# An output-projection schedule at a kernel's end: three old output tiles moved ahead, between conv and gating groups

## The chip, the cores and the metric

The kernel runs on all 8 cores of one Trainium2 chip. Each core takes one prompt sequence of 2048 tokens and 64 of the 512 sample tokens; the cores share nothing and exchange nothing. The metric is the device time of the slowest core in microseconds (us). In every core TensorE (PE) multiplies matrices, VectorE (DVE), ScalarE (ACT) and GpSimd (POOL) do the elementwise work, and SyncE (SP) issues most DMAs of activations. Each engine executes its own instructions strictly in the order in which the program lists them and waits on semaphores for results of the others.

## The reference, cut to what matters

```python
h = rms_norm(x, g_norm) * (1 + scale) + shift          # shift, scale, gate from silu(c) @ w_ada + b_ada
p = h @ w_in                                           # (T, 1024) @ (1024, 3584)
h_a, b_a, c_a, z_a, u_b, v_b, z_b = split(p)           # seven pieces of width 512
s = c_a * h_a                                          # group A: short gated convolution
conv = w[0] * s[t-2] + w[1] * s[t-1] + w[2] * s[t]
y_a = b_a * conv * silu(z_a)
v_n = layer_norm(v_b)                                  # group B: spatial gating, chunks of 128 positions
y_b = u_b * (tril(w_s) @ v_n + b_s) * silu(z_b)
y = concat([y_a, y_b]) @ w_out                         # (T, 1024) @ (1024, 1024)
out = rms_norm(x + gate * y, g_final)
# further outputs: the last two rows of s (new conv state), v_n of the sample tokens
```

## The kernel before

The 16 tiles of 128 prompt tokens of a core, and one tile of 64 sample tokens, are worked off in five blocks: `BLOCKS = ((4, False), (4, False), (3, True), (3, False), (2, False))`, tiles and whether the sample tile is in it. The last block (index 4) has two tiles, so its matmuls stream 256 columns; block 3, `PV` there, has three tiles.

Activations are kept transposed: `hT` holds 8 slices of 128 features. For a block the program records, in this order:
- four conv groups j = 0 to 3 (`A1`, `A2`). `A1` multiplies h and C (8 matmuls each, L477); ACT copies h out of its bank (L506), DVE forms s (L514), ACT takes the first tap (L525), DVE the other two (L532, twice). `A2` multiplies B and z; DVE gates (L546), ACT takes the silu (L550), POOL writes slice j of `yT` (L551).
- `V`: the v projection with its layer norm (L592, L607 to L622), within the conv groups; in the last block behind group 1.
- four gating groups (`GB`): U and z matmuls (16, L477), silu on ACT (L644), product on DVE (L647), the mixing matmuls (L656), their scaling on DVE (L666), and POOL writes slice 4 + j of `yT` (L676).

The output projection runs one block late. For an old tile, `C_mm` is 16 matmuls of 512 columns into two banks (L704); `C_s1` multiplies by the gate (DVE, L720 and L721) and adds x (DVE, L723; x comes by a DMA into `xc`, recorded by `C_load`, all three at once by `first_c`); `C_sq` sums the squares on ACT (L733); `C_s2` makes the reciprocal root in two steps on one number per row, L791 and then POOL's power (L793); `C_s3` scales the tile on DVE (L802) and SP stores it (L317). `cq` is the list of tiles of which `C_s3` is still to come; at the start of the last block a prompt tile of block 2 and its sample tile are in it.

In the last block before the change, old tile j (j = 0, 1, 2) goes behind gating group j. Then come the block's own two tiles: tile 0 (`C_mm` over slices 0 to 6 and then slice 7, `C_s1`, `C_s2`, `C_s3`), and tile 1 in two halves of 512 output columns (L743, `C_end1` L759 and L761, squares L763, `C_end2` L774, L776, L781), whose stores end the kernel. A `C_mm` over slices 0 to 6 is one recorded step: it waits at its first matmul until all seven slices are there.

The order on each engine is this recorded order; there is no planner. The recorder `Sched` adds a semaphore wait wherever a step reads or overwrites what another engine's step wrote or reads. Banks (8), `tmp` (9), `xc` (3) and `ob` (3, the output tiles) are handed out in rotation.

Of the kernel before, what the change touches and what calls it, by code (L numbers as in the profile page):

```python
# [7 lines left out]
ALU = mybir.AluOpType  # L8
AF = mybir.ActivationFunctionType

EPS = 1e-6
NCORES = 8
D = 1024
# [177 lines left out]
def build_nc(limit=None):  # L191
# [36 lines left out]
    def op(eng, fn, r=(), w=(), dma=False):  # L228
        return S.op(eng, fn, reads=r, writes=w, dma=dma)
# [96 lines left out]
    for b, (nt, smp) in enumerate(BLOCKS):  # L326
        B = Blk()
# [250 lines left out]
    def V2():  # L578
        while vlate:
            vlate.pop(0)()  # L580
# [202 lines left out]
               r=[("oh", n), sres, "gf_bc"], w=[("oh", n)])  # L783
            store(y_p[rows, sl], o[:, sl], [("oh", n)], ("out_y", B.i, i, n))

    def C_s2(B, i):
        ti, P, kind = B.tiles[i]
        R = slice(64, 128) if kind == "s" else slice(0, 128)
        o, ores, st, sres = cst[(B.i, i)]
        ss, rs = st[:, 0:1], st[:, 1:2]  # L790
        op("dve", lambda e: e.tensor_scalar(out=rs, in0=ss, scalar1=1.0 / D, scalar2=EPS, op0=ALU.mult, op1=ALU.add),  # L791
           r=[sres], w=[sres])
        op("pool", lambda e: e.tensor_tensor(out=rs, in0=rs, in1=mhalf[:, 0:1], op=ALU.pow),  # L793
           r=[sres, "mhalf"], w=[sres])
# [151 lines left out]
    cq = []  # L946
# [12 lines left out]
    def nxp(f, i, *a):  # L959
        if NX is not None and i < len(NX.tiles):  # L960
            f(NX, i, *a)

    for b in range(nb):
        B = PB[b]
        NX = PB[b + 1] if b + 1 < nb else None
        PV = PB[b - 1] if b > 0 else None
        N2 = PB[b + 2] if b + 2 < nb else None
        npv = len(PV.tiles) if PV is not None else 0
        last = NX is None
        late = b < 2  # L970

        def first_c():
            for i in range(min(NXC, npv)):
                C_load(PV, i)

        if last:
            for i in range(len(B.tiles)):
                C_load(B, i, i)
        for j in range(4):
            if not late:  # L980
                if j < 2:
                    nxp(prep_load, j + 2)
            A1(B, j)
            if b == 0 and j == 3:
                V2()
            if not late:
                nxp(prep_sq, j + 1)
            elif j == 3 and b == 1:
                nxp(prep_sq, 2)
                nxp(prep2, 0, "act")  # L990
            if j < 2 and cq and not last:
                C_s3(*cq.pop(0))
                if cq:
                    C_s2(*cq[0])
            A2(B, j)
            if last and j == 2 and cq:
                C_s3(*cq.pop(0))
                if cq:
                    C_s2(*cq[0])
            if not late:  # L1000
                nxp(prep2, j, "act")
                nxp(prep_xn, j + 1)
            if b == 0 and j == 0:
                late_loads_1([("spadB", 0)])
            if b == 1 and j == 0:
                wblk_ops()
            if j == 2 and b > 1:
                first_c()
            if b == 1 and j == 2:
                nxp(prep_sq, 0)  # L1010
                nxp(prep_sq, 1)
            if j == (1 if last else 2):
                V(B, (lambda: nxp(prep_xn, 0)) if b == 1 else None)
                if b > 0:
                    V2()
            if b == 0 and j == 2:
                wt_ops()
            if b == 0 and j == 3:
                nxp(prep_sq, 0)
                nxp(prep_sq, 1)  # L1020
                bias2_ops()
                nxp(prep_xn, 0)
                nxp(prep_xn, 1)
            if b == 1 and j == 2:
                nxp(prep_xn, 1)
                nxp(prep_load, 2)
                nxp(prep_load, 3)
            if b == 1 and j == 3:
                nxp(prep2, 1, "act")
                nxp(prep_xn, 2)  # L1030
        if not late and N2 is not None:
            for i in range(2):
                prep_load(N2, i)
        if b == 1:
            gate_ada()
            for q in range(NXC):
                S.alias(("xc", q), [("wada", 0), ("wada", 1), ("wada", 2), ("xa", 4), ("xa", 5)])
            for q in range(NOB):
                S.alias(("o", q), [("wada", 0), ("wada", 1), ("wada", 2), ("xa", 4), ("xa", 5)])
            first_c()  # L1040
        if not last:
            newconv(B)
        for j in range(4):
            if last:
                GB(B, j, (lambda j=j: C_sq(PV, j - 1)) if 0 < j <= npv else None)
                if j > 0:
                    C_s2(PV, j - 1)
                if j < npv:
                    C_mm(PV, j, 0, 8)
                    C_s1(PV, j, False)  # L1050
                if j == 0:
                    newconv(B)
                    while cq:
                        C_s3(*cq.pop(0))
                elif j < 4:
                    C_s3(PV, j - 1)
                continue
            if not late and not last:
                prep3(NX, [2 * j, 2 * j + 1])
            if b == 1 and j == 0:  # L1060
                nxp(prep_sq, 3)
            if b == 1 and j >= 2:
                prep3(NX, range(4 * j - 8, 4 * j - 4), "both")
            if j == 3 and N2 is not None and b > 0:
                prep_xn(N2, 0)
            GB(B, j)
            if b == 0 and j == 1:
                nxp(prep2, 0, "act")
                nxp(prep2, 1, "dve")
                nxp(prep_sq, 2)  # L1070
                nxp(prep_sq, 3)
                nxp(prep_xn, 2)
                nxp(prep_xn, 3)
            if b == 0 and j == 2:
                nxp(prep2, 2, "act")
                nxp(prep2, 3, "dve")
                prep3(NX, range(8), "both")
            if b == 1 and j < 2:
                nxp(prep2, 2 + j, "act")
                if j == 0:  # L1080
                    nxp(prep_xn, 3)
                prep_load(N2, j)
            if j < npv:
                C_step(PV, j, (PV, j + NXC) if j + NXC < npv else None)
            if j == 2 and N2 is not None and b > 0:
                prep_sq(N2, 0)
        if b == 0:
            for k in range(8):
                S.alias(("yT", 1, k), [("wada", 3), ("xa", 6), ("xa", 7)])
            late_loads_2([("win", 22, 0)])  # L1090
        if last:
            C_mm(B, 0, 0, 7)
            C_mm(B, 0, 7, 8)
            C_s1(B, 0)
            C_mm_half(B, 1, 0)
            C_end1(B, 1, 0)
            C_s2(B, 0)
            C_mm_half(B, 1, 1)
            C_end1(B, 1, 1)
            C_s3(B, 0)  # L1100
            C_end2(B, 1)
# [60 lines left out]
```

How the kernel before makes its waits and increments, by code:

```python
        def run(e, eng):  # L113
            seen = {}
            nw = 0
            for o in streams[e]:
                need = {}
                waits = list(o.deps)
                if o.is_dma and o.prev is not None:
                    waits.append(o.prev)
                for d in waits:
                    key = d.sem.num
                    if key not in need or need[key][1] < d.val:
                        need[key] = (d.sem, d.val)
                for key, (sem, val) in need.items():
                    if seen.get(key, 0) >= val:
                        continue
                    eng.wait_ge(sem, val)
                    seen[key] = val
                    nw += 1
                ins = o.fn(eng)
                if o.is_dma:
                    ins.then_inc(o.sem, 16)
                elif o.needed:
                    ins.then_inc(o.sem, 1)
            stats[e] = (len(streams[e]), nw)
# [18 lines left out]
            @block.sync  # L155
            def _(eng):
                run("sp", eng)
                for q in self.QUEUES:
                    last = {}
                    for o in streams[q]:
                        if o.is_dma:
                            last[o.sem.num] = (o.sem, o.val)
                    for sem, val in last.values():
                        eng.wait_ge(sem, val)
```

## Time and profile before

| | us |
|---|---|
| median of 3 runs (lowest, highest) | 343.68 (343.39, 365.61) |
| the profiled execution | 343.48 |
| its span on the slowest core (6), and on the fastest (1) | 341.7 and 338.1 |
| PE busy in the span | 287.9 (84%) |
| DVE busy | 186.5 (55%) |
| ACT busy | 122.0 (36%) |
| POOL busy | 110.6 (32%) |

The profile is of one execution, on its slowest core. The span runs from that core's first to its last instruction; 1.8 us of the execution's time lie around it. Times in rows are us from the span's start. Matmuls are pipelined, so a row of PE gives a group from its first start to its last end, and groups overlap by some 0.2 us. Neighbouring instructions of DVE likewise overlap by up to 0.1 us; where a sum is made, the distance from start to start is what counts.

### The profile page before, as it was taken

To read this page: it belongs to the slowest core of one execution; us is meant where nothing else is said; L and a number is where in the kernel's file an instruction comes from. 1 tells how busy PE (TensorE), PEld (TensorE's weight loads), DVE (VectorE), ACT (ScalarE), POOL (GpSimd) and SP (SyncE) were. 2 spreads that over 40 slices of the span, in tenths; PEclk is the share of its full clock that TensorE was granted. 3 is DMA by queue.
4 is the path that set the end of the run, shared out by engine and by line. 5 is a ranking of instruction groups with operands and counts; after the bars stand their busy time and mean duration, and the time that the engine had idled before them with its cause. 6 is when DMAs were issued, how large, how long until landed. Compare 5 with 4: busy or idle time off the path is not lost.

```text
span 341.7 us, 5602 instructions; the slowest of 8 cores (338.1 to 341.7 us)
## 1 busy us (share of the span) xinstructions
PE 287.9 (84%) x1767; PEld 151.4 (44%) x1792; DVE 186.5 (55%) x350; ACT 122.0 (36%) x215; POOL 110.6 (32%) x161
## 2 busy tenths in 40 slices
PE   0324639997799999999999999999999999999840
PEld 0222324443444445444455454446555557765410
DVE  0321015444564454846778836468863666667982
ACT  2611024207452234723445262443415244232320
POOL 7293065214423431412226342121432112222210
PEclk9999959999999999999999999999999999999995
DMA  5999999999999973193122715111180102527223
GB/s 130 214 166 165 170 160 146 176 160 257 204 213 182 228 131 94 31 255 118 62 92 93 205 44 149 61 63 62 61 238 11 33 0 94 154 70 195 90 111 124
DMA packets 14157, 44.51 MB, mean 130 GB/s; under 512 B 1968, under 2 KB 2352, under 8 KB 13104
## 3 DMA queue, kind: packets, MB, share of 16 engines
q0 software_dynamic: 6624, 21.24, 34.7%
q1 hardware_dynamic: 7504, 22.91, 22.2%
q8 instruction: 15, 0.25, 0.3%
q14 instruction: 14, 0.11, 0.1%
HBM read 51.02 MB, written 8.85 MB: 175 GB/s over the span
## 4 chain that ended last, share of the span: by engine, by line
PE 54%; DMA 24%; DVE 9%; issue 6%; POOL 3%; ACT 2%; DVEq 1%; POOLq 0%; SPq 0%; ACTq 0%
PE pb L477 31%; PE pb L704 12%; DMA win_bf<-win_l 12%; DMA wada<-wada_l 10%; PE pb L592 7%; DMA xc<-x_p 2%; DVE ob L802 2%; PE pb L403 2%; PE pb L656 1%; PE pb L814 1%; POOL xa L314 1%; DVE ob L723 1%; DVE tmp L532 1%; DVE ob L720 1%; DVE ob L721 1%
## 5 line engine op out<-in xcount | busy, mean ns | idle before, releaser
L477 PE MATMUL pb<-hT,win_bf 128*128 128x512 bf16 (+3 forms) x672 | 125.6, 341 | 4.1 <-DVE hT L410 1.8
L477 PEld LDWEIGHTS pb<-hT,win_bf 128*128 128x128 bf16 x680 | 66.0, 98 | 59.1 <-issue 4.9
L704 PE MATMUL pb<-wout_bf,yT 128*128 128x512 bf16 (+1 forms) x246 | 56.8, 379 | 2.7 <-POOL yT L676 1.2
L477 PE MATMUL pb<-hT,wh 128*128 128x512 bf16 (+3 forms) x277 | 53.9, 355 | 3.6 <-ACT hT L419 3.6
L676 POOL TENSOR_TENSOR yT<-tmp,tmp 128x512 bf16<-128x512 f32 (+3 forms) x20 | 22.0, 1098 | 67.7 <-DVE tmp L666 37.0
L551 POOL TENSOR_TENSOR yT<-tmp,tmp 128x512 bf16<-128x512 f32 (+3 forms) x20 | 23.7, 1185 | 58.0 <-DVE tmp L546 41.1
L733 ACT ACTIVATE junk<-ob 128x1024 bf16<-128x1024 f32 (+1 forms) x16 | 16.9, 1057 | 71.5 <-DVE ob L723 58.7
L477 PEld LDWEIGHTS pb<-hT,wh 128*128 128x128 bf16 x280 | 27.7, 100 | 27.9 <-issue 7.9
L532 DVE SCALAR_TENSOR_TENSOR tmp<-spad,pv,tmp 128x512 f32<-128x512 f32 (+2 forms) x40 | 26.3, 658 | 20.3 <-ACT tmp L525 13.1
L704 PEld LDWEIGHTS pb<-wout_bf,yT 128*128 128x128 bf16 (+1 forms) x256 | 23.9, 98 | 29.3 <-issue 2.4
L592 PE MATMUL pb<-wv_bf,hT 128*128 128x512 bf16 (+1 forms) x133 | 29.6, 379 | 0.2
L419 ACT ACTIVATE hT<-hT,shT,aT 128x384 bf16<-128x384 bf16 (+2 forms) x28 | 18.0, 694 | 26.3 <-DVE aT L468 25.4
L525 ACT ACTIVATE tmp<-spad,pv 128x512 f32<-128x512 f32 (+2 forms) x20 | 12.7, 636 | 38.4 <-DVE spad L514 29.7
L389 DVE TENSOR_SCALAR xn<-xa,stat 128x1024 bf16<-128x1024 f32 (+1 forms) x17 | 12.8, 755 | 24.5 <-POOL stat L382 24.4
L403 PE MATMUL pb<-ident,xn 128*128 128x128 bf16 (+1 forms) x136 | 11.5, 238 | 16.9 <-DVE xn L389 16.9
L514 DVE TENSOR_TENSOR spad<-pb,tmp 128x512 f32<-128x512 f32 (+2 forms) x20 | 11.7, 585 | 22.5 <-PE pb L477 11.0
L647 DVE TENSOR_TENSOR tmp<-pb,tmp 128x512 f32<-128x512 f32 (+3 forms) x20 | 11.9, 595 | 19.7 <-ACT tmp L644 19.7
L802 DVE SCALAR_TENSOR_TENSOR ob<-ob,stat,gf_bc 128x1024 f32<-128x1024 f32 (+1 forms) x16 | 20.5, 1280 | 1.5 <-POOL stat L793 1.4
L723 DVE TENSOR_TENSOR ob<-ob,xc 128x1024 f32<-128x1024 f32 (+1 forms) x15 | 18.4, 1225 | 4.7 <-DMA xc<-x_p 2.4
L378 ACT ACTIVATE junk<-xa 128x1024 bf16<-128x1024 f32 (+1 forms) x17 | 17.9, 1053 | 7.4 <-DMA xa<-x_p 7.0
L592 PEld LDWEIGHTS pb<-wv_bf,hT 128*128 128x128 bf16 (+1 forms) x136 | 13.3, 99 | 15.6 <-issue 0.4
L622 ACT ACTIVATE vn_bf<-pb,stat 128x512 bf16<-128x512 f32 x16 | 11.2, 774 | 24.2 <-DVE stat L616 12.8
(88 smaller groups left out, 261.1 us busy)
## 6 DMA issues: line engine op xcount, KB each, us to landing
y_p<-ob SPq DMA_DIRECT2D x15, 512.0 KB, 2.7
xc<-x_p SPq DMA_DIRECT2D x14, 512.0 KB, 7.8
wada<-wada_l POOLq DMA_DIRECT2D x6, 1024.0 KB, 36.0
xa<-x_p POOLq DMA_DIRECT2D x10, 512.0 KB, 40.1
win_bf<-win_l POOLq DMA_DIRECT2D x17, 256.0 KB, 43.5
xa<-x_p SPq DMA_DIRECT2D x8, 512.0 KB, 6.6
wout_bf<-wout_l POOLq DMA_DIRECT2D x2, 1024.0 KB, 60.4
wh<-winh_l POOLq DMA_DIRECT2D x4, 256.0 KB, 27.5
```

What stands on the lines that cost most here:

```text
L378: op("act", lambda e: e.activation(out=junk[0:P, :], in_=xa[ra][0:P, :], func=AF.Square, accum_out=ss), r=[("xa", ra)], w=[sres, "junk"])
L403: ii = pe.transpose(out=tv[:, k, 0:P], in_=xn[rn][0:P, k * 128:(k + 1) * 128], identity=ident[0:P, 0:P])
L419: op("act", lambda e, k=k: e.activation(out=hb[:, k, 0:B.NP], in_=hb[:, k, 0:B.NP], func=AF.Identity, scale=aT[:, k, 0:1], bias=shT[:, k, ...
L477: ii = pe.matmul(bk.t[:, 0:B.N], lhsT=wsl(m, k), rhs=hT[B.h][:, k, 0:B.N], start=(k == 0), stop=(k == 7))
L532: ii = e.scalar_tensor_tensor(out=o[:, 0:NP], in0=spad[j][:, tp:tp + NP], scalar=cw(j, tp), in1=a[:, 0:NP], op0=ALU.mult, op1=ALU.add)
L551: op("pool", lambda e: e.tensor_tensor(out=yT[B.y][:, j, 0:N], in0=c2[:, 0:N], in1=sg[:, 0:N], op=ALU.mult), r=[c2r, sgr], w=[("yT", B.y, j)])
L592: ii = pe.matmul(bk.t[0:P, :], lhsT=hT[B.h][:, k, ti * 128:ti * 128 + P], rhs=wv_bf[:, k, :], start=(k == 0), stop=(k == 7))
L676: op("pool", lambda e: e.tensor_tensor(out=yT[B.y][:, 4 + j, 0:N], in0=tU[:, 0:N], in1=mb[:, 0:N], op=ALU.mult), r=[tUr, mbr], w=[("yT", B ...
L704: ii = pe.matmul(bk.t[R, :], lhsT=yT[B.y][:, k, ti * 128:ti * 128 + P], rhs=wout_bf[:, n, k, :], start=(k == 0), stop=(k == 7))
L723: op("dve", lambda e: e.tensor_tensor(out=o[R, :], in0=o[R, :], in1=xt[R, :], op=ALU.add), r=[ores, xr], w=[ores])
L733: op("act", lambda e: e.activation(out=junk[R, :], in_=o[R, :], func=AF.Square, accum_out=st[R, 0:1]), r=[ores], w=[sres, "junk"])
L802: op("dve", lambda e: e.scalar_tensor_tensor(out=o[R, :], in0=o[R, :], scalar=rs, in1=gf_bc[R, :], op0=ALU.mult, op1=ALU.mult), r=[ores, s ...
```

## The change

Old tile 0 goes behind conv group 2, old tile 1 behind conv group 3, old tile 2 behind gating group 0; gating groups 1, 2 and 3 stand in a row. The three loads of x for them are recorded behind conv group 1 in place of conv group 2. The small step L791 goes from DVE to POOL for the three old tiles and the block's tile 0. The square sums, the scalings L802 and the four small copies L565 (the conv state, `newconv`) move along.

```diff
--- before.py
+++ after.py
@@ -783,12 +783,12 @@
                r=[("oh", n), sres, "gf_bc"], w=[("oh", n)])
             store(y_p[rows, sl], o[:, sl], [("oh", n)], ("out_y", B.i, i, n))
 
-    def C_s2(B, i):
+    def C_s2(B, i, eng="dve"):
         ti, P, kind = B.tiles[i]
         R = slice(64, 128) if kind == "s" else slice(0, 128)
         o, ores, st, sres = cst[(B.i, i)]
         ss, rs = st[:, 0:1], st[:, 1:2]
-        op("dve", lambda e: e.tensor_scalar(out=rs, in0=ss, scalar1=1.0 / D, scalar2=EPS, op0=ALU.mult, op1=ALU.add),
+        op(eng, lambda e: e.tensor_scalar(out=rs, in0=ss, scalar1=1.0 / D, scalar2=EPS, op0=ALU.mult, op1=ALU.add),
            r=[sres], w=[sres])
         op("pool", lambda e: e.tensor_tensor(out=rs, in0=rs, in1=mhalf[:, 0:1], op=ALU.pow),
            r=[sres, "mhalf"], w=[sres])
@@ -988,15 +988,22 @@
             elif j == 3 and b == 1:
                 nxp(prep_sq, 2)
                 nxp(prep2, 0, "act")
+            if last and j == 3:
+                C_sq(PV, 0)
             if j < 2 and cq and not last:
                 C_s3(*cq.pop(0))
                 if cq:
                     C_s2(*cq[0])
             A2(B, j)
-            if last and j == 2 and cq:
-                C_s3(*cq.pop(0))
+            if last and j >= 2:
                 if cq:
-                    C_s2(*cq[0])
+                    C_s3(*cq.pop(0))
+                    if cq:
+                        C_s2(*cq[0])
+                C_mm(PV, j - 2, 0, 8)
+                if j == 3:
+                    C_s2(PV, 0, "pool")
+                C_s1(PV, j - 2, False)
             if not late:
                 nxp(prep2, j, "act")
                 nxp(prep_xn, j + 1)
@@ -1004,7 +1011,7 @@
                 late_loads_1([("spadB", 0)])
             if b == 1 and j == 0:
                 wblk_ops()
-            if j == 2 and b > 1:
+            if j == (1 if last else 2) and b > 1:
                 first_c()
             if b == 1 and j == 2:
                 nxp(prep_sq, 0)
@@ -1042,18 +1049,19 @@
             newconv(B)
         for j in range(4):
             if last:
-                GB(B, j, (lambda j=j: C_sq(PV, j - 1)) if 0 < j <= npv else None)
-                if j > 0:
-                    C_s2(PV, j - 1)
-                if j < npv:
-                    C_mm(PV, j, 0, 8)
-                    C_s1(PV, j, False)
+                GB(B, j, (lambda j=j: C_sq(PV, j + 1)) if j < 2 else None)
                 if j == 0:
+                    C_s3(PV, 0)
+                    C_mm(PV, 2, 0, 8)
+                    C_s2(PV, 1, "pool")
+                    C_s1(PV, 2, False)
+                elif j == 1:
+                    C_s3(PV, 1)
                     newconv(B)
-                    while cq:
-                        C_s3(*cq.pop(0))
-                elif j < 4:
-                    C_s3(PV, j - 1)
+                elif j == 2:
+                    C_s2(PV, 2, "pool")
+                else:
+                    C_s3(PV, 2)
                 continue
             if not late and not last:
                 prep3(NX, [2 * j, 2 * j + 1])
@@ -1094,7 +1102,7 @@
             C_s1(B, 0)
             C_mm_half(B, 1, 0)
             C_end1(B, 1, 0)
-            C_s2(B, 0)
+            C_s2(B, 0, "pool")
             C_mm_half(B, 1, 1)
             C_end1(B, 1, 1)
             C_s3(B, 0)
```

On PE, from the v projection (L592) of the last block on. L477 are projections, L704 an output tile, L656 the mixing of a gating group. Before:

```order
 L592 MATMUL pb<-wv_bf,hT_47 128x512 x16
 L477 MATMUL pb<-hT_47,win_bf 128x256 x80
 L656 MATMUL pb<-Wt,vn_bf_89 64x128 x2
 L656 MATMUL pb<-Wt,vn_bf_90 64x128 x2
 L704 MATMUL pb<-wout_bf,yT_115 128x512 x16
 L477 MATMUL pb<-hT_47,win_bf 128x256 x16
```

And with the change:

```order
 L592 MATMUL pb<-wv_bf,hT_47 128x512 x16
 L477 MATMUL pb<-hT_47,win_bf 128x256 x32
 L704 MATMUL pb<-wout_bf,yT_115 128x512 x16
 L477 MATMUL pb<-hT_47,win_bf 128x256 x32
 L704 MATMUL pb<-wout_bf,yT_115 128x512 x16
 L477 MATMUL pb<-hT_47,win_bf 128x256 x16
```

The 80 projections of conv groups 2 and 3 and gating group 0 now have the first two old tiles between them; what is left of the list is the same number of instructions.

On DVE, from the scaling of the tile before the sample tile (ob_113) into conv group 3 (L510 to L546), in the change:

```order
 L802 SCALAR_TENSOR_TENSOR ob_113<-ob_113,stat,gf_bc 128x1024
 L791 TENSOR_SCALAR stat<-stat 128x1
 L720 TENSOR_TENSOR ob_112<-pb,gate_p 128x512
 L721 TENSOR_TENSOR ob_112<-pb,gate_p 128x512
 L723 TENSOR_TENSOR ob_112<-ob_112,xc_109 128x1024
 L510 COPY spad_57<-spad_57 128x2
 L514 TENSOR_TENSOR spad_57<-pb,tmp_97 128x256
```

L720, L721 and L723 of old tile 0 are new here; before, L510 followed L791 at once, and they stood behind gating group 0.

On DVE, gating groups 2 and 3 (L647, L666) and the start of the last block's tile 0 (ob_112), before:

```order
 L802 SCALAR_TENSOR_TENSOR ob_112<-ob_112,stat,gf_bc 128x1024
 L647 TENSOR_TENSOR tmp_99<-pb,tmp_98 128x256
 L666 SCALAR_TENSOR_TENSOR tmp_100<-pb,pv,bias_68 128x256
 L791 TENSOR_SCALAR stat<-stat 128x1
 L720 TENSOR_TENSOR ob_114<-pb,gate_p 128x512
 L721 TENSOR_TENSOR ob_114<-pb,gate_p 128x512
 L723 TENSOR_TENSOR ob_114<-ob_114,xc_111 128x1024
 L802 SCALAR_TENSOR_TENSOR ob_113<-ob_113,stat,gf_bc 128x1024
 L647 TENSOR_TENSOR tmp_102<-pb,tmp_101 128x256
 L666 SCALAR_TENSOR_TENSOR tmp_103<-pb,pv,bias_68 128x256
 L791 TENSOR_SCALAR stat<-stat 128x1
 L802 SCALAR_TENSOR_TENSOR ob_114<-ob_114,stat,gf_bc 128x1024
```

And with the change:

```order
 L802 SCALAR_TENSOR_TENSOR ob_113<-ob_113,stat,gf_bc 128x1024
 L565 COPY ncp_sb<-spad_54 128x2
 L565 COPY ncp_sb<-spad_55 128x2
 L565 COPY ncp_sb<-spad_56 128x2
 L565 COPY ncp_sb<-spad_57 128x2
 L647 TENSOR_TENSOR tmp_99<-pb,tmp_98 128x256
 L666 SCALAR_TENSOR_TENSOR tmp_100<-pb,pv,bias_68 128x256
 L647 TENSOR_TENSOR tmp_102<-pb,tmp_101 128x256
 L666 SCALAR_TENSOR_TENSOR tmp_103<-pb,pv,bias_68 128x256
 L802 SCALAR_TENSOR_TENSOR ob_114<-ob_114,stat,gf_bc 128x1024
```

Nothing stands between the two groups any more; the four copies now stand ahead of group 2.

## Rows read from the trace of the kernel before

**Rows 1.** Timeline of PE: start, us, engine, line, operation, idle before and its releaser.

```profile
294.55 8.90 PE L477 MATMUL pb<-hT,win_bf 128*128 128x256 bf16 x80
...
320.14 0.30 PE L656 MATMUL pb<-Wt,vn_bf 128*64 128x128 bf16 x4
321.01 2.97 PE L704 MATMUL pb<-wout_bf,yT 128*128 128x512 bf16 x13 [0.57 <-POOL stat L793]
325.15 0.59 PE L704 MATMUL pb<-wout_bf,yT 128*128 128x512 bf16 x2 [1.17 <-POOL yT L676]
325.58 3.61 PE L743 MATMUL pb<-wout_bf,yT 128*128 128x512 bf16 x16
```

**Rows 2.** Timeline of DVE, conv group 3 to old tile 0 (same columns).

```profile
302.62 0.42 DVE L546 TENSOR_TENSOR tmp<-pb,tmp 128x256 f32<-128x256 f32 x1
302.96 1.27 DVE L802 SCALAR_TENSOR_TENSOR ob<-ob,stat,gf_bc 128x1024 f32<-128x1024 f32 x1
...
304.22 0.62 DVE L510 COPY spad<-spad 128x2 f32<-128x2 f32 x1
304.95 0.42 DVE L514 TENSOR_TENSOR spad<-pb,tmp 128x256 f32<-128x256 f32 x1
...
307.31 0.42 DVE L546 TENSOR_TENSOR tmp<-pb,tmp 128x256 f32<-128x256 f32 x1
...
311.31 1.23 DVE L723 TENSOR_TENSOR ob<-ob,xc 128x1024 f32<-128x1024 f32 x1 [1.65 <-DMA xc<-x_p]
312.45 0.37 DVE L565 COPY ncp_sb<-spad 128x2 f32<-128x2 f32 x4
```

**Rows 3.** Chain of waits that ended last: start, us, what, from 302 us.

```profile
304.75 6.47 DMA xc<-x_p
```

**Rows 4.** Timeline of DVE, gating groups 2 and 3 (same columns).

```profile
318.75 0.42 DVE L647 TENSOR_TENSOR tmp<-pb,tmp 128x256 f32<-128x256 f32 x1
...
319.54 0.68 DVE L720 TENSOR_TENSOR ob<-pb,gate_p 128x512 f32<-128x512 f32 x1
...
322.13 1.28 DVE L802 SCALAR_TENSOR_TENSOR ob<-ob,stat,gf_bc 128x1024 f32<-128x1024 f32 x1
323.33 0.42 DVE L647 TENSOR_TENSOR tmp<-pb,tmp 128x256 f32<-128x256 f32 x1
```

**Rows 5.** Timeline of DVE, the last two output tiles (same columns).

```profile
325.62 1.28 DVE L802 SCALAR_TENSOR_TENSOR ob<-ob,stat,gf_bc 128x1024 f32<-128x1024 f32 x1 [1.42 <-POOL stat L793]
326.82 0.69 DVE L720 TENSOR_TENSOR ob<-pb,gate_p 128x512 f32<-128x512 f32 x1
...
331.11 0.15 DVE L791 TENSOR_SCALAR stat<-stat 128x1 f32<-128x1 f32 x1 [0.28 <-ACT junk L733]
...
332.62 1.28 DVE L802 SCALAR_TENSOR_TENSOR ob<-ob,stat,gf_bc 128x1024 f32<-128x1024 f32 x1
...
334.76 1.42 DVE L781 SCALAR_TENSOR_TENSOR ob<-ob,stat,gf_bc 128x512 f32<-128x512 f32 x2 [0.80 <-POOL stat L776]
```

**Rows 6.** Timeline of POOL (same columns).

```profile
303.25 1.57 POOL L551 TENSOR_TENSOR yT<-tmp,tmp 128x256 bf16<-128x256 f32 x1 [5.24 <-DVE tmp L546]
...
324.28 0.72 POOL L676 TENSOR_TENSOR yT<-tmp,tmp 128x256 bf16<-128x256 f32 x1 [3.34 <-DVE stat L791]
...
331.41 0.55 POOL L793 TENSOR_TENSOR stat<-stat,mhalf 128x1 f32<-128x1 f32 x1 [5.90 <-DVE stat L791]
```

**Rows 7.** Timeline of ACT, a sum of squares (same columns).

```profile
317.79 1.06 ACT L733 ACTIVATE junk<-ob 128x1024 bf16<-128x1024 f32 x1 [2.79 <-DVE ob L723]
```

**Rows 8.** All instructions of POOL's small step L380: durations min/median/max in ns.

```profile
L380 POOL TENSOR_SCALAR stat<-stat x17: 183/191/560, 9.7 to 239.4; 128x1 f32<-128x1 f32 x16, 64x1 f32<-64x1 f32 x1
```

**Rows 9.** Timeline of PE early in the kernel (same columns).

```profile
41.09 0.98 PE L450 MATMUL pb<-silucT,wada 128*128 128x17 bf16 x32 [2.18 <-DMA wada<-wada_l]
```

**Rows 10.** Windows: busy us of PE, PEld, DVE, ACT, POOL, granted clock, DMA share, GB/s.

```profile
41.00:42.00 1.00, 0.91 (x32) 0.91 (x32) 0.00 (x0) 0.00 (x0) 0.00 (x0) 0.82 0.94 180
48.00:52.00 4.00, 2.67 (x7) 1.11 (x9) 1.01 (x4) 2.11 (x3) 3.83 (x8) 0.52 1.03 164
331.00:332.00 1.00, 0.00 (x0) 0.00 (x0) 0.80 (x2) 0.73 (x3) 0.55 (x1) 0.88 0.00 0
```

## The prediction

> **What bounds the kernel now.** The share of busy time says PE (84% of the span), so I read its timeline for the last block first. From the v projection to the last mixing step PE hardly pauses. Then it waits 0.57 us before the last block's tile 0 and 1.17 us for slice 7 of `yT`, and its last matmul ends at 325.58 + 3.61 = 329.19 [rows 1]. The span goes on to 341.7. So at the end somebody else is late. The chain of waits passes from DVE's scaling through the load of x for old tile 0 (304.75, 6.47 us) and back to DVE [rows 3], then stays on DVE. DVE's timeline shows why. Old tile 0 waits 1.65 us for its x [rows 2]. From there DVE has no pause until L666 of group 3, so the product L647 of group 3 comes at 323.33, though its matmuls ended before 320.2 [rows 1, 4]. Next DVE idles 1.42 us for the power of old tile 2, starts L720 of tile 0 at 326.82, and ends at 334.76 + 1.42 = 336.18 [rows 5]. The limit of this stretch is DVE's list, and PE's waits follow from it.
>
> **How I sum.** All work up to 302.62 (L546 of conv group 2) stands as before on DVE, ACT and POOL. From there I walk DVE's new list with distances from start to start of the same steps, in the profiled execution (343.48 us; the median, 343.68, is 0.2 above it). The distances: L546 to L802 0.34 [rows 2]; L647, L666 and L791 together 0.79, of which I give L791 0.06 as an estimate from its 0.15 and the usual overlap, so 0.73 without it [rows 4, 5]; L720, L721, L723 together 322.13 - 319.54 = 2.59; L802 323.33 - 322.13 = 1.20 [rows 4].
>
> **Old tiles 0 and 1 move behind conv groups 2 and 3.** PE reaches tile 0 after 32 of the 80 projections, 294.55 + 32 x 0.11 = 298.1, and is through it at about 301.6 (3.61 a tile, less the overlap) [rows 1]. Nothing waits for PE there: DVE starts L720 only after L802 and L791, at about 304.2 [rows 2]. Its x is there too. The load is now recorded ahead of the store that held it back to 304.75; the loads of x ahead of it on SP's queue are issued at the block's start, over 10 us earlier, and even 6.47 us of flight [rows 3] from PE's arrival at 294.55 ends before 305.6. **The wait of 1.65 us goes.** What it costs instead: L510 of conv group 3 stands behind these 2.59 us, at 306.8. Before, L510 took 0.62 us, and L514 came 0.73 after it; there POOL was still busy until 303.25 + 1.57 = 304.82 [rows 2, 6]. That overlap is gone, and I take 0.27 (between 0.15 and 0.73). So L514 comes at 307.1, L546 2.36 later [rows 2] at 309.4, the sample tile's L802 at 309.8, old tile 1 at 311.0, and L647 of gating group 0 at 313.6. PE is hidden from this delay: conv group 3's matmuls lie in banks that PE takes again only for old tile 2, by then at 310.7, and B's is free at 309.4 + 0.42. That cover is 0.9 us thick; any delay over it is PE's, though PE has slack there as shown next.
>
> **Old tile 2 behind group 0, groups 1 to 3 in a row.** Group 0 and L802 of old tile 0: 313.6 + 0.73 + 1.20 = 315.5. Old tile 2: 318.1. Group 1 and L802 of old tile 1: 320.0. Here the four copies L565 take 0.37 alone [rows 2], with the step to the next 0.40. Group 2's L647 then comes at 320.4.
>
> **The copies' place.** L551 of POOL, started 0.29 us after an L802, took 1.57 us against 0.72 for the like L676 [rows 6], and ended 0.59 after that L802; the copy L510 started meanwhile ended as POOL ended [rows 2]. In the new order group 1 repeats this: POOL's L676 comes 0.95 after L647 (324.28 - 323.33 [rows 4, 6]), so at 319.0, inside L802, ends near 320.7, and the copies behind it are held until then. I take 0.6 us for it, since the place is built like the row: L647 of group 2 at 321.0. The bounds are 0 and 0.85, what L551 lost. The Trainium skill (SBUF — State Buffer, section on the two separate sides) calls the port pair shared by DVE and GpSimd an exclusive lock, taken for a whole instruction. By that rule the 0.6 is due in full; if only bandwidth were shared, the sum would be lower by up to 0.6.
>
> **What PE then meets.** POOL writes slice 6 at 321.0 + 0.95 = 321.95, and PE starts 0.87 after such a start (325.15 - 324.28 [rows 1, 6]), at 322.8. PE has the same instructions ahead of it as before and is ready at 320.4, so it waits 2.4 us in one piece: the 0.57 and 1.17 us come back as this. Slice 7: L647 at 321.7, and POOL meanwhile has L791 and L793 of old tile 2 ahead of it. It should be written by 324.6; PE needs it 14 matmuls after 322.8, near 325.9. No second wait. The tile ends at 322.8 + (325.15 + 0.59 - 321.01) - 1.17 = 326.4, against 325.74 before.
>
> **The end.** Old tile 2's L802 is done by 325.6, so L720 of tile 0 starts as PE ends, 326.5, against 326.82: **0.3 us gained**. Behind it L791 leaves DVE, with its wait of 0.28 for the squares and some 0.1 of its own: **0.4 us gained** [rows 5]. On POOL such a step lasts 0.19 to 0.56 us [rows 8], with a hand-over of 0.15 as an estimate. Before, the power ended at 331.96 and L802 started at 332.62 [rows 5, 6]. The reserve of 0.66 just covers both the step and the earlier need. If it doesn't, up to 0.3 of the gain is lost. ACT's squares of old tile 2 (1.06 and a short read-out [rows 7]) now stand ahead of group 2's silu and end near 319.7. The silu is then done near 320.1, before DVE asks for it.
>
> **Sum:** 1.65 (x) + 0.46 (L510's wait) + 1.42 (power of old tile 2, now hidden behind PE) are removed from DVE, and most return as DVE waiting for PE, which waits for DVE's slice 6. The end moves by -0.3 - 0.4 = -0.7. **343.48 - 0.7 = 342.8 us.** With the copies not held it is 342.2, with L791 late and the copies at their worst 343.3.
>
> **Rivals.**
> *No pause ahead of tile 0.* If DVE were through group 2 some 2 us earlier than I sum, PE would run on at 320.6 and finish tile 0 at 324.1. The tail follows 2.4 earlier than in my sum: 340.4 us, or 341.6 halfway. For it speaks that DVE loses two waits. Against it speak the distances: they hold no idle time that could go, and DVE has the same old tiles ahead of group 2.
> *Nothing gained.* The powers L793 (0.55 us each [rows 6]) now fall beside L723 of old tiles 1 and 2, both reading SBUF. If each of three holds DVE up for half its length, 0.8 us is added ahead of slice 6: 343.6 us.
> *The clock falls in the new pause: slower.* Early on PE paused 2.18 us, then ran 32 small matmuls, and the granted clock fell from 1.00 (0.82 in that window) to half, 1.2 GHz [rows 9, 10]. At the end it still stood at full, 2.4 GHz, until the window 331 to 332, over 2 us behind the last matmul [rows 1, 10]. The price by rows: seven matmuls of 512 columns took 2.67 us before the clock came back, 0.38 each against 3.61 / 16 = 0.23, so 1.1 us, or 32 x 0.15 = 4.9 if it stays down through the last three pieces. That gives 343.9 to 347.7 us. It decides from a pause of about 2.2 us; mine is 2.4, but with full work on both sides, where the row had little. The Trainium skill (TensorE: Matmul & The Clock Gate, Part 1) names the same two levels and says the low one follows idle time.
> *It doesn't do what it says.* The order of instructions shows both moves on PE and DVE. Only the early load could fail, if x came late; that gives back up to 1.65 us on DVE, 344.
>
> **How the numbers follow.** My sum 0.60; no pause, wholly or half, 0.12; nothing gained 0.16; clock 0.10; late x 0.02. The range takes my sum's bounds, the nothing-gained case, half of the no-pause case and the lower end of the clock's: 341.2 to 344.1. 2% of this kernel is 6.9 us, about what a measurement can tell from no change; no case reaches it downwards, and upwards none within its priced bounds. So 0.01 faster, 0.98 same, 0.01 slower.
>
> **What would show it.** In the changed profile: L723 of old tile 0 without a wait for x; L510 of conv group 3 near 306.8 and 0.16 us long; copies L565 long, POOL's L676 of group 1 at 1.5 us; one PE pause near 2.4 us ahead of tile 0, ended by POOL, and none for slice 7; no L791 ahead of the second L759. I am wrong if that pause is under 1 us, if the tail from L720 on isn't shorter than 9.36 us, or if the clock falls in 320 to 330.

## The result and the profile after

The changed kernel is **slower**: 346.44 us median (344.61 to 348.83) against 343.64 for the kernel before in the same comparison. The ratio is 1.0076, with a 95% interval of 1.0058 to 1.0094: 2.6 us. The ratio leaves out executions in which a whole die ran at a lower granted clock, such as the one of 365.61 us before, so it is not quite the quotient of the medians. The forecast was 342.8, the range 341.2 to 344.1. The profiled execution took 345.02 us.

The slowest core of it, the fastest and a third, with span and mean granted clock; before, the slowest core had 341.7 us:

```profile
core 2: 343.5 us, clock 0.961
core 3: 342.1 us, clock 0.966
...
core 6: 343.1 us, clock 0.962
```

PE of the changed kernel on its slowest core, 2, against [rows 1]; columns as there. Core 2 runs 0.42 us ahead of core 6 of before at conv group 2's L546 (302.20 against 302.62 [rows 2]), so 0.42 is added where times are compared.

```profile
297.64 3.62 PE L704 MATMUL pb<-wout_bf,yT 128*128 128x512 bf16 x15
...
304.59 3.62 PE L704 MATMUL pb<-wout_bf,yT 128*128 128x512 bf16 x15
...
319.59 0.30 PE L656 MATMUL pb<-Wt,vn_bf 128*64 128x128 bf16 x4
323.25 5.08 PE L704 MATMUL pb<-wout_bf,yT 128*128 128x512 bf16 x15 [3.36 <-POOL stat L791]
328.18 3.62 PE L743 MATMUL pb<-wout_bf,yT 128*128 128x512 bf16 x16
```

The two waits of before, 0.57 and 1.17 us, are one of 3.36 us. And tile 0's 16 matmuls, which take 3.62 us at full clock (see the like row of 304.59), take 5.08. The trace lacks one record of the 16 in each of these rows. In the row of tile 0 it is the first: on the cores with all 16, tile 0 starts 26.45 us after the norm step L610, on core 2 26.67. So the pause of core 2 is really some 3.14 us and tile 0 lasts 5.30; on the cores with all 16 the pauses are 3.11 to 3.33. The row of before with 13 records [rows 1] has the same flaw: there PE waited 0.3 to 0.4 us, as on the cores with all 14. The granted clock by microseconds (the first of a row's last three numbers) shows why:

```profile
322.00:323.00 1.00, 0.00 (x0) 0.00 (x0) 0.53 (x2) 0.00 (x0) 0.87 (x2) 1.00 0.60 217
...
324.00:325.00 1.00, 1.00 (x4) 0.39 (x3) 1.00 (x1) 0.00 (x0) 0.34 (x1) 0.50 0.00 0
...
327.00:328.00 1.00, 1.00 (x6) 0.48 (x5) 0.00 (x0) 0.00 (x0) 0.00 (x0) 0.93 0.67 266
```

It stood at 1.00 up to 323, in the pause, was at half, 1.2 GHz, in 324 to 325 with the matmuls running again, and was back to nearly full in 327 to 328. It fell on all eight cores, on five in the pause and on three within 0.7 us of the matmuls' return. On core 6 the same matmuls took 6.52 us:

```profile
317.89 0.30 PE L656 MATMUL pb<-Wt,vn_bf 128*64 128x128 bf16 x4
321.40 6.52 PE L704 MATMUL pb<-wout_bf,yT 128*128 128x512 bf16 x16 [3.20 <-POOL stat L791]
```

DVE of the changed kernel, core 2, against [rows 2, 4, 5]:

```profile
302.20 0.42 DVE L546 TENSOR_TENSOR tmp<-pb,tmp 128x256 f32<-128x256 f32 x1
...
305.25 1.23 DVE L723 TENSOR_TENSOR ob<-ob,xc 128x1024 f32<-128x1024 f32 x1 [0.17 <-DVE ob L721]
306.39 0.16 DVE L510 COPY spad<-spad 128x2 f32<-128x2 f32 x1
307.01 0.42 DVE L514 TENSOR_TENSOR spad<-pb,tmp 128x256 f32<-128x256 f32 x1 [0.46 <-DVE spad L510]
...
309.38 0.42 DVE L546 TENSOR_TENSOR tmp<-pb,tmp 128x256 f32<-128x256 f32 x1
309.83 1.29 DVE L802 SCALAR_TENSOR_TENSOR ob<-ob,stat,gf_bc 64x1024 f32<-64x1024 f32 x1
311.15 0.69 DVE L720 TENSOR_TENSOR ob<-pb,gate_p 128x512 f32<-128x512 f32 x1
...
320.19 0.90 DVE L565 COPY ncp_sb<-spad 128x2 f32<-128x2 f32 x4
321.00 0.41 DVE L647 TENSOR_TENSOR tmp<-pb,tmp 128x256 f32<-128x256 f32 x1
...
323.75 1.67 DVE L802 SCALAR_TENSOR_TENSOR ob<-ob,stat,gf_bc 128x1024 f32<-128x1024 f32 x1 [1.22 <-POOL stat L793]
328.51 0.69 DVE L720 TENSOR_TENSOR ob<-pb,gate_p 128x512 f32<-128x512 f32 x1 [3.09 <-PE pb L704]
...
336.15 1.41 DVE L781 SCALAR_TENSOR_TENSOR ob<-ob,stat,gf_bc 128x512 f32<-128x512 f32 x2 [0.80 <-POOL stat L776]
```

L723 of old tile 0 (305.25) has no wait for x. Tile 0's L720 waits 3.09 us for PE, where before DVE was the late one. POOL, core 2, against [rows 6]:

```profile
319.23 1.63 POOL L676 TENSOR_TENSOR yT<-tmp,tmp 128x256 bf16<-128x256 f32 x1 [1.91 <-DVE tmp L666]
321.95 0.73 POOL L676 TENSOR_TENSOR yT<-tmp,tmp 128x256 bf16<-128x256 f32 x1 [1.09 <-DVE tmp L666]
322.76 0.19 POOL L791 TENSOR_SCALAR stat<-stat 128x1 f32<-128x1 f32 x1
...
323.61 0.72 POOL L676 TENSOR_TENSOR yT<-tmp,tmp 128x256 bf16<-128x256 f32 x1
```

For the experiments I use one more measure, **the last stretch**: from the start of the norm step L610 of the last block on DVE to the end of the last L781, on each core of the profiled execution. It leaves out the start of the kernel, which varies from core to core. Before, it is 39.19 us on the slowest core (296.99 to 336.18), 38.1 to 38.2 on the three cores where x of old tile 0 was late by 0.22 us at most, up to 39.8 elsewhere; the median of the cores is 39.1. With the change it is 40.98 on core 2 (296.58 to 337.56), 40.6 to 41.0 on six more and 42.21 on core 6.

### The profile page after: what moved, and what is told of

It is laid out like the page before. It is cut to its first block, busy times and chain, and to the rows that moved or that the text cites. A ratio compares the mean times of both kernels' runs of the same rounds, so it can differ in the third digit from the quotient of the medians.

```text
span 343.5 us, 5602 instructions; the slowest of 8 cores (342.1 to 343.5 us)
## 1 busy us (share of the span) xinstructions
PE 290.5 (85%) x1767; PEld 152.2 (44%) x1792; DVE 187.4 (55%) x346; ACT 121.7 (35%) x215; POOL 114.3 (33%) x165
## 4 chain that ended last, share of the span: by engine, by line
PE 57%; DMA 23%; DVE 7%; issue 5%; POOL 3%; ACT 1%; DVEq 1%; ACTq 0%; POOLq 0%
PE pb L477 30%; PE pb L704 17%; DMA win_bf<-win_l 12%; DMA wada<-wada_l 11%; PE pb L592 7%; PE pb L403 1%; PE pb L656 1%; PE pb L814 1%; POOL xa L314 1%; DVE tmp L532 1%; DVE ob L723 1%; DVE ob L802 1%; DVE ob L720 1%; DVE ob L721 1%; DVE spad L514 0%
## 5 line engine op out<-in xcount | busy, mean ns | idle before, releaser
L477 PE MATMUL pb<-hT,win_bf 128*128 128x512 bf16 (+3 forms) x672 | 125.9, 341 | 2.0 <-DMA win_bf<-win_l 1.4
L477 PEld LDWEIGHTS pb<-hT,win_bf 128*128 128x128 bf16 x680 | 65.9, 98 | 57.0 <-issue 2.4
L704 PE MATMUL pb<-wout_bf,yT 128*128 128x512 bf16 (+1 forms) x246 | 58.4, 388 | 4.2 <-POOL stat L791 3.4
L477 PE MATMUL pb<-hT,wh 128*128 128x512 bf16 (+3 forms) x277 | 54.8, 359 | 3.7 <-ACT hT L419 3.6
L551 POOL TENSOR_TENSOR yT<-tmp,tmp 128x512 bf16<-128x512 f32 (+3 forms) x20 | 24.7, 1236 | 63.7 <-DVE tmp L546 39.5
L676 POOL TENSOR_TENSOR yT<-tmp,tmp 128x512 bf16<-128x512 f32 (+3 forms) x20 | 23.8, 1188 | 59.7 <-DVE tmp L666 41.5
L477 PEld LDWEIGHTS pb<-hT,wh 128*128 128x128 bf16 x280 | 28.0, 101 | 28.6 <-issue 9.0
L704 PEld LDWEIGHTS pb<-wout_bf,yT 128*128 128x128 bf16 (+1 forms) x256 | 24.6, 100 | 31.6 <-issue 5.5
L592 PE MATMUL pb<-wv_bf,hT 128*128 128x512 bf16 (+1 forms) x133 | 29.6, 379 | 0.2
L525 ACT ACTIVATE tmp<-spad,pv 128x512 f32<-128x512 f32 (+2 forms) x20 | 12.7, 636 | 40.2 <-DVE spad L514 31.5
L514 DVE TENSOR_TENSOR spad<-pb,tmp 128x512 f32<-128x512 f32 (+2 forms) x20 | 11.7, 584 | 24.1 <-PE pb L477 12.3
L647 DVE TENSOR_TENSOR tmp<-pb,tmp 128x512 f32<-128x512 f32 (+3 forms) x20 | 11.9, 593 | 18.8 <-ACT tmp L644 18.6
L802 DVE SCALAR_TENSOR_TENSOR ob<-ob,stat,gf_bc 128x1024 f32<-128x1024 f32 (+1 forms) x16 | 20.9, 1303 | 1.3 <-POOL stat L793 1.2
L723 DVE TENSOR_TENSOR ob<-ob,xc 128x1024 f32<-128x1024 f32 (+1 forms) x15 | 18.4, 1225 | 3.6 <-DVE ob L721 2.4
L592 PEld LDWEIGHTS pb<-wv_bf,hT 128*128 128x128 bf16 (+1 forms) x136 | 13.3, 99 | 15.6 <-issue 0.4
```

The source lines that it names most:

```text
L477: ii = pe.matmul(bk.t[:, 0:B.N], lhsT=wsl(m, k), rhs=hT[B.h][:, k, 0:B.N], start=(k == 0), stop=(k == 7))
L551: op("pool", lambda e: e.tensor_tensor(out=yT[B.y][:, j, 0:N], in0=c2[:, 0:N], in1=sg[:, 0:N], op=ALU.mult), r=[c2r, sgr], w=[("yT", B.y, j)])
L592: ii = pe.matmul(bk.t[0:P, :], lhsT=hT[B.h][:, k, ti * 128:ti * 128 + P], rhs=wv_bf[:, k, :], start=(k == 0), stop=(k == 7))
L676: op("pool", lambda e: e.tensor_tensor(out=yT[B.y][:, 4 + j, 0:N], in0=tU[:, 0:N], in1=mb[:, 0:N], op=ALU.mult), r=[tUr, mbr], w=[("yT", B ...
L704: ii = pe.matmul(bk.t[R, :], lhsT=yT[B.y][:, k, ti * 128:ti * 128 + P], rhs=wout_bf[:, n, k, :], start=(k == 0), stop=(k == 7))
L723: op("dve", lambda e: e.tensor_tensor(out=o[R, :], in0=o[R, :], in1=xt[R, :], op=ALU.add), r=[ores, xr], w=[ores])
```

## The experiments

Ratios are to the kernel before on the same chip; the median of that kernel was 341.9 to 344.2 us from group to group of runs, so only ratios and last stretches are compared between groups.

| run | ratio (95% interval) | last stretch, median of cores, us |
|---|---|---|
| the change | 1.0076 (1.0058 to 1.0094) | 40.9 |
| fill12 | 0.9986 (0.9967 to 1.0006) | 39.2 |
| fill6 | 1.0005 (0.9986 to 1.0024) | 39.2 |
| copies_late | 0.9995 (0.9975 to 1.0015) | 40.2 |
| split | 0.9943 (0.9922 to 0.9963) | 37.8 |
| split_copies | 0.9965 (0.9946 to 0.9985) | 37.3 |
| split_l791_dve | 0.9978 (0.9955 to 1.0001) | 37.9 |
| best | 0.9927 (0.9901 to 0.9953) | 36.8 |
| before_early_x | 0.9947 (0.9925 to 0.9969) | 38.2 |
| before_early_x_again | 0.9970 (0.9951 to 0.9990) | 38.2 |
| before_merge | 1.0137 (1.0105 to 1.0168) | 43.5 |
| merge_fill18 | 1.0054 (1.0032 to 1.0075) | 41.1 |

### Filling the pause (fill12, fill6)

```diff
+            fill(12)          # fill(6) in the second
             C_mm(B, 0, 0, 7)
```

`fill(n)` issues n matmuls of 512 columns on PE into tile 0's first bank, which tile 0 then overwrites.

> The changed kernel, with 12 matmuls of 512 columns added on PE in front of the last block's tile 0; their result is never used and they wait for nothing late. Theory 1, the granted clock: the pause of 3.3 us ahead of tile 0 makes the clock fall, and tile 0's 16 matmuls run at half rate. With 2.6 us of other matmuls in the pause the clock stays at full; tile 0 takes some 3.5 us in place of 5.1, its end and all behind it come 1.6 us or more earlier, and the time is 342.8 to 343.3 us, a little under the kernel before. Theory 2, the queue of DVE alone: slice 6 comes late because DVE's list is longer, and the clock has no part; then the filling changes nothing, 346 to 346.5 us.

PE of fill12 on its slowest core, 3:

```profile
319.05 2.76 PE L953 MATMUL pb<-wout_bf,yT 128*128 128x512 bf16 x12
322.15 3.61 PE L704 MATMUL pb<-wout_bf,yT 128*128 128x512 bf16 x16 [0.34 <-POOL yT L676]
325.60 3.62 PE L743 MATMUL pb<-wout_bf,yT 128*128 128x512 bf16 x16
```

Tile 0 is back at 3.61 us. In the profiled execution the clock fell on no core before the end of the matmuls, and all eight last stretches are 39.2. The time is that of the kernel before (ratio 0.9986, with 1 inside its interval), at 343.13 us. This is theory 1: DVE's and POOL's lists are those of the change, PE's list has only the 12 matmuls more, the clock stays, and 1.4 to 1.8 us of the last stretch go on seven cores (3.0 on core 6). Of that, 0.1 is that tile 0 starts 26.35 us after L610 in place of 26.45; the rest, 1.3 to 1.7 us and 2.9 on core 6, is the length of tile 0's matmuls. That is the price of the clock. The run also puts a number on the change without its clock: no gain and no loss.

> As the run with 12 added matmuls, but with 6: 1.3 us of work at the front of the pause, so that 2.0 us of it stay empty. Theory 1, clock: shorter pauses make it fall on fewer cores (2.3 us still made it fall on six of eight). If 2.0 us is short enough, 343.2 us as with 12; if it falls on some cores in some executions, 343.5 to 345 us. A pure queue effect would give 346 us, which the run with 12 has already spoken against.

```profile
320.17 1.24 PE L953 MATMUL pb<-wout_bf,yT 128*128 128x512 bf16 x5 [0.16 <-issue]
323.05 3.61 PE L704 MATMUL pb<-wout_bf,yT 128*128 128x512 bf16 x16 [1.63 <-POOL yT L676]
```

(PE, core 2; one record of six is missing.) With six matmuls an empty pause of 1.63 us is left. The clock did not fall there on any core of the profiled execution; the last stretch is 39.2 on seven cores and 39.35 on core 6. The ratio, 1.0005, agrees with fill12 within the intervals.

### The copies behind group 3 (copies_late)

```diff
                 elif j == 1:
                     C_s3(PV, 1)
-                    newconv(B)
...
                 else:
                     C_s3(PV, 2)
+                    newconv(B)
```

> The changed kernel, with the four copies of the conv state (L565) and their store moved behind gating group 3 and old tile 2's scaling. They took 0.9 us on DVE ahead of group 2, held by POOL. Slice 6 comes 0.8 to 0.9 us earlier and the pause ahead of tile 0 shrinks from 3.3 to 2.5 us. Theory 1, clock: the clock falls in some executions and cores only, so more than 0.9 comes off on the median: 343 to 345 us. Theory 2, queue alone: 0.9 off, 345.5 us.

```profile
322.55 0.36 DVE L565 COPY ncp_sb<-spad 128x2 f32<-128x2 f32 x4
```

(DVE, core 2.) The four copies take 0.36 us here, against 0.90 at 320.19 in the change, where POOL's L676 ran from 319.23 to 320.86. PE then pauses 2.3 to 2.4 us (rows of 2.5 and 2.6 on cores 0 and 6, where the first record is missing). On two cores, 3 and 7, the clock stayed at full; on the other six it fell. Tile 0 on core 2, then on core 3:

```profile
320.24 5.30 PE L704 MATMUL pb<-wout_bf,yT 128*128 128x512 bf16 x16 [2.33 <-POOL stat L791]
```

```profile
321.29 3.61 PE L704 MATMUL pb<-wout_bf,yT 128*128 128x512 bf16 x16 [2.33 <-POOL stat L791]
```

Both pauses are 2.33 us, the last stretches 40.16 and 38.47: **1.7 us for the clock, with the same program and the same pause**. The gain over the change is 2.8 us by the ratios (1.0076 to 0.9995, give or take 0.9), where the copies themselves are worth 0.8 (L802 to group 2's L647: 2.00 us in the change, 1.20 here). So more than the queue went, as theory 1 said. The rest is not split up further. The time is that of the slowest of eight cores, so one core with a long low spell can set it. The 20 executions of the change point that way: in five of them the slowest core had a mean granted clock of 0.952 to 0.957, and these five took 346.9 to 348.8 us, all above the median. In the executions of the kernel before that the ratios count, the slowest core was never below 0.964.

### Tile 0 in four steps (split)

```diff
-            C_mm(B, 0, 0, 7)
+            C_mm(B, 0, 0, 5)
+            C_mm(B, 0, 5, 6)
+            C_mm(B, 0, 6, 7)
             C_mm(B, 0, 7, 8)
```

> The changed kernel, with tile 0's output projection recorded in four steps (slices 0 to 4, 5, 6, 7) in place of two (0 to 6, 7), the same 16 matmuls in the same order. Both theories: ten matmuls run at once at 319.9, the rest follow slices 5, 6 and 7, written at 320.9, 322.7 and 324.3, so the tile is done near 325.0 and DVE begins it at 325.5 behind old tile 2's scaling. Theory 1, clock: pauses of at most 1.5 us with matmuls between, the clock stays: 3 us or more off, 341.5 to 342.2 us. Theory 2, no clock effect in the slowdown: the tile at full rate would end 326.8 in place of 325.0, so the gain over the change is near 1.8 less, 344 to 345 us.

PE, core 1:

```profile
318.57 2.76 PE L704 MATMUL pb<-wout_bf,yT 128*128 128x512 bf16 x12
321.57 0.59 PE L704 MATMUL pb<-wout_bf,yT 128*128 128x512 bf16 x2 [0.23 <-POOL yT L676]
323.23 0.59 PE L704 MATMUL pb<-wout_bf,yT 128*128 128x512 bf16 x2 [1.07 <-POOL yT L676]
```

Twelve matmuls run at once, the rest follow their slices with pauses of 0.23 and 1.07 us. The clock stays and the tile is done 3 us earlier. I had expected ten at once: slice 5 was there in time too. 0.9943: faster than the kernel before, and 4.6 us faster than the change. The last stretch fell by 3.1. Against fill12, where the clock stays too, it is 1.4 shorter: that part is work done in the pause, the rest the clock.

### One part alone: the early loads (before_early_x, twice)

```diff
-            if j == 2 and b > 1:
+            if j == (1 if last else 2) and b > 1:
                 first_c()
```

This is the kernel before with only that line.

> The kernel before, with one part of the change alone: the three loads of x recorded behind conv group 1 in place of 2. The wait of 1.65 us of old tile 0 goes. If DVE's queue is what sets the end, as predicted, slice 7 comes 1.1 to 1.6 us earlier, the pause of 1.17 us shrinks, and the end moves by -1.0 to -1.3: near 342.5 us. If the load was hidden anyway: 343.6 us.

DVE, core 3:

```profile
309.19 1.23 DVE L723 TENSOR_TENSOR ob<-ob,xc 128x1024 f32<-128x1024 f32 x1 [0.17 <-DVE ob L721]
...
323.96 1.28 DVE L802 SCALAR_TENSOR_TENSOR ob<-ob,stat,gf_bc 128x1024 f32<-128x1024 f32 x1 [1.42 <-POOL stat L793]
```

L723 of old tile 0 has lost its wait of 1.65 us; the wait of 1.42 for the power stays. All eight last stretches are 38.1 to 38.2: 1.0 less than before on the slowest core. The ratio 0.9947 says 1.8 us, more than that. So it was run again on another chip:

> The kernel before with the early loads alone, again, for a comparison on the same chip as the version above. By the last stretch (38.17 us there) it should be 0.9 to 1.2 us slower than that version, and 0.9 to 1.6 faster than the kernel before on the cores where x came late.

0.9970, and the same 38.2: 1.0 us. Before, the cores where x was late had 39.0 to 39.8, so the slowest of the eight gains the most. What else lies between the two ratios stays open.

### The price of the small step L791 (split_l791_dve)

All four `"pool"` arguments of `C_s2` taken out of split.

> The version with tile 0 in four steps, with one part of the change undone: the small step L791 back on DVE for the three old tiles and tile 0. Predicted gain of that part: 0.4 us, from the wait of 0.28 us and the step itself ahead of tile 1's second half. On DVE the step for old tile 2 stands right behind group 3, so POOL has one step less ahead of slice 7: that can give back 0.3. Expected 341.4 to 341.7 us against 341.25; the rival, that POOL's extra step costs more than DVE's wait, gives 340.9.

DVE, core 1:

```profile
320.38 0.14 DVE L791 TENSOR_SCALAR stat<-stat 128x1 f32<-128x1 f32 x1
...
321.94 1.67 DVE L802 SCALAR_TENSOR_TENSOR ob<-ob,stat,gf_bc 128x1024 f32<-128x1024 f32 x1 [0.70 <-POOL stat L793]
...
327.90 0.15 DVE L791 TENSOR_SCALAR stat<-stat 128x1 f32<-128x1 f32 x1 [0.23 <-ACT junk L733]
```

Both expected effects are there. Old tile 2's L802 waits 0.70 us for the power in place of 1.22. At the end L791 waits 0.23 us for the squares, ahead of the second L759. They cancel: 37.87 against 37.80. The ratio 0.9978 (on another chip) doesn't resolve it.

### The same clock in the kernel before (before_merge, merge_fill18)

```diff
-            C_mm(B, 0, 0, 7)
-            C_mm(B, 0, 7, 8)
+            C_mm(B, 0, 0, 8)
```

> The kernel before, with tile 0's output projection in one step (slices 0 to 7) in place of two. Nothing of DVE's or POOL's list changes. PE pauses from 320.4 to 325.6, 5.1 us, and DVE begins tile 0 at 329.2 in place of 326.8. Without a clock effect that is +2.4: 346.0 us. Theory 1, clock: it falls in the pause, the tile's 16 matmuls and some of the next run at half rate, 1.7 to 3.4 us more: 347.7 to 349.4 us.

PE, core 7:

```profile
324.01 6.31 PE L704 MATMUL pb<-wout_bf,yT 128*128 128x512 bf16 x16 [4.92 <-POOL yT L676]
```

The pause is 4.92 us there, 4.0 to 4.9 on the six cores with all 16 records, and tile 0 takes 6.31 us. 1.0137 is 4.7 us, of which 2.4 were expected without the clock.

> The kernel before with tile 0's output projection in one step, and 18 unused matmuls (3.9 us) on PE in the pause of 4 to 5 us ahead of it. DVE's and POOL's lists are those of before. Clock theory: the pause left is near 1 us, the clock stays, and the last stretch (from the norm step L610 to the end of L781) is shorter than in the run without filling by the clock's price, 1.6 us or more: some 41 us in place of 42.1 to 44.2. If the pause itself, and not the clock, set the time there, nothing changes.

PE, core 7:

```profile
320.88 4.06 PE L953 MATMUL pb<-wout_bf,yT 128*128 128x512 bf16 x18
325.76 3.61 PE L704 MATMUL pb<-wout_bf,yT 128*128 128x512 bf16 x16 [0.83 <-POOL yT L676]
```

3.61 us again, and 1.0054: 1.9 us of the 4.7 stay. The last stretches are 40.35 to 41.8 in place of 42.1 to 44.2. Both ranges are wide since x was late by a different time on each core; on core 5, where it wasn't late in either run, it is 40.4 in place of 42.1. DVE's and POOL's lists are those of the kernel before in both. So the clock's fall needs nothing of the change but the pause.

### The versions that came out (split_copies, best)

> Both improvements on the changed kernel: tile 0 in four steps, and the four copies behind group 3. With the clock at full, DVE's list sets the end: group 2 comes 0.9 us earlier, old tile 2's power and its scaling too, and tile 0's first step on DVE with them. 341.25 - 0.9 = 340.4 us. If PE bounds the end by then, it gives 341.0 us.

The last stretch is 37.27, 0.5 less than split's 37.80, where 0.9 was expected: tile 0 is bound by slice 7 then, with PE waiting 0.66 us for it, and the copies' 0.3 us now stand right ahead of L720. The ratio doesn't confirm this gain: 0.9965, where split had 0.9943 on another chip, with intervals that overlap.

```diff
                 elif j == 2:
-                    C_s2(PV, 2, "pool")
+                    C_s2(PV, 2)
```

> The version in four steps with the copies behind group 3, and L791 of old tile 2 alone back on DVE, so that POOL has one step less ahead of slice 7. L720 of tile 0 should come 0.2 to 0.3 us earlier, the last stretch 37.0 us against 37.27. If POOL's step was covered there: 37.3 us.

PE and then DVE, core 7:

```profile
319.18 3.19 PE L704 MATMUL pb<-wout_bf,yT 128*128 128x512 bf16 x14
322.74 0.59 PE L704 MATMUL pb<-wout_bf,yT 128*128 128x512 bf16 x2 [0.37 <-POOL yT L676]
```

```profile
322.01 1.67 DVE L802 SCALAR_TENSOR_TENSOR ob<-ob,stat,gf_bc 128x1024 f32<-128x1024 f32 x1 [0.69 <-POOL stat L793]
...
323.88 0.68 DVE L720 TENSOR_TENSOR ob<-pb,gate_p 128x512 f32<-128x512 f32 x1
```

All eight last stretches are 36.8: 2.4 us less than the kernel before on its slowest core, 4.1 less than the change. Expected were 37.0. Slice 7's wait is down from split_copies' 0.66 us to 0.37. The ratio is 0.9927 (0.9901 to 0.9953), 2.5 us, the fastest version by its estimate; its interval overlaps those of split and before_early_x. Against before_early_x_again on the same chip it is 341.50 to 343.13 us by the medians, and 1.36 us by the last stretch. So the moved tiles are worth something once the pause is cut up.

## Why the prediction was wrong

**The step that failed is the end of tile 0.** The sum let its 16 matmuls run at the full clock, from 322.8 to 326.4, and left the clock's fall to a rival with a chance of 0.10. The clock fell in that pause or just behind it on all eight cores, and the matmuls took 5.30 us on core 2 in place of 3.61. The rival, "The clock falls in the new pause: slower", had the right place (ahead of tile 0), a condition that was met (a pause of about 2.2 us; mine was 2.4) and a price, 343.9 to 347.7 us, that holds the 346.44. By its own condition it should have been the likeliest case. I held against it that full work stood on both sides of the pause, where the early row had little; the runs show that this is no protection. fill12 shows the cause, copies_late the price at one and the same pause, and before_merge with merge_fill18 the same in another kernel. The price was 1.3 to 1.7 us on seven cores and 2.9 on core 6.

The trace of before could have said so. The prediction gives the clock behind the last matmul on core 6 alone, where it stood for over 2 us. On core 1 the last matmuls, with PE busy all through, end at 325.63, and the window from 328 is already at half:

```profile
322.01 3.62 PE L743 MATMUL pb<-wout_bf,yT 128*128 128x512 bf16 x16
328.00:329.00 1.00, 0.00 (x0) 0.00 (x0) 0.90 (x2) 0.25 (x2) 0.39 (x1) 0.50 0.00 0
```

So the clock fell there within 2.4 us of full work. On the other cores of before it took 2.5 to over 4 us: what one core shows is not what all eight do.

**The pause was sized too small**, 2.4 us against the 3.14 of core 2. It starts as predicted (320.4, measured 319.89 + 0.42 = 320.3). It ends later by two terms. DVE's list is 0.42 late at group 2's L647 (321.00 + 0.42 against 321.0): L514 followed L510 after 0.62 us, with 0.46 idle, where I took 0.27; L802 followed L546 after 0.45 in place of 0.34; the sample tile's L802 took 1.32 to the next start in place of 1.20. These make 0.58. The copies gave some back: with their hold they took 0.81 us to the next start, where I had 1.00. The other term is 0.21: on the cores with all 16 records PE began 1.08 us after the start of POOL's slice 6, where I took 0.87 from slice 7's row. (Core 2's row says 1.30, of which 0.22 is the missing record.) The hand-over from the end of POOL's write was 0.35 us there, and 0.36 on the cores of before with all 14 records. It was 0.15 for slice 7 before, and for slices 6 and 7 in split. Tile 0's first matmul is the start of a step that waits for banks as well as slices; that this makes the difference is not shown.

**The sum of core 2**, against the forecast: 0.42 for DVE's list, 0.21 for the hand-over, 1.7 for the clock, 0.1 between tile 0's matmuls and DVE, 0.1 in the tail: 2.5 us. The median is missed by 3.6, since the profiled execution was one of the faster ones of the change; no trace shows a slower one.

**The sum without the clock** was -0.7 and is 0.0: fill12's last stretch is 39.19 where core 6 of before had 39.19. There DVE's list accounts for 0.42, the hand-over (0.26 with the matmuls ahead) for 0.12, and the two last terms for 0.1 each.

**Right:** the wait for x went. The copies were held by POOL, 0.90 us against 0.37, though by less than the 0.6 forecast, and POOL's L676 of group 1 took 1.63. There was one pause ahead of tile 0 and none for slice 7. The tail from L720 on took 9.05 us against 9.36 (8.96 forecast); L791 had left it. ACT's squares did not hold up DVE. DVE was the limit up to slice 6, as argued; what it cost was PE's clock.

**The rival of no pause** needed DVE 2 us earlier, which did not come. What that rival missed is that the pause could be cut up without touching DVE, by splitting the wait of `C_mm`: slices 0 to 4 were there at once and slice 5 soon after (split). **Nothing gained** named the size of the change without its clock, for the wrong reason: no power held up L723.

The change and its parts, then: early loads -1.0 us on the slow cores' last stretch; moving the tiles takes that back, through the longer way to slice 6; the pause costs 1.3 to 2.9 in clock. The median loses 2.6. The longer way is this: group 2's L647 comes 24.42 us after L610 in the change and 20.28 in before_early_x, while group 3's, 25.15 against 25.3, hardly moves. The change gathered DVE's work ahead of slice 6, which tile 0's first step waits for, and freed only the time behind it.

## What to carry to other kernels

Before gathering PE's small waits into one, count what the single pause does to the granted clock: if a row of the trace shows a fall after a pause of that size, on any core, take it as the likeliest case, whatever work stands around it. A matmul group that waits for all its inputs at its first matmul makes such a pause; split its wait by input, and the same work fills it. Size a hand-over from a row with the same waits, not from a neighbour's, and count the records of the row first: a missing first record reads as 0.2 us of waiting.

## What the runs showed of the hardware

- The clock and the pause, ahead of 16 matmuls of 512 columns, with PE fully busy before it: empty pauses of 1.62 to 1.82 us, a fall on none of 8 cores (fill6); 2.32 to 2.42 us, on 6 of 8 (copies_late); 3.11 to 3.33 us, on 8 of 8 (the change), each in one profiled execution and on cores with all records. The fall came in the pause or within 1.2 us of the matmuls' return. Cores with the same 2.33 us came out differently (copies_late, 2 and 3).
- VectorE and GpSimd hold each other up both ways. L676 took 1.63 us beside an L802 that had started first (319.23, L802 at 319.00) against 0.73 beside L647 and L666 (321.95). L802 took 1.67 beside an L676 that had started first (323.61, L802 at 323.75), against 1.28. The copies L565 took 0.90 against 0.36. The Trainium skill (SBUF — State Buffer, section on the two separate sides) describes this as an exclusive lock of a shared port pair, held by whichever instruction starts first; the rows agree: in each pair the one that started later took longer, and the first copy, begun within L676, lasted 0.69 us and ended with it.
- The small step on GpSimd lasted 0.19 us and was 0.34 ahead of the next instruction, the lower end of [rows 8].
